# Moving the first half of one projection ahead of the last modulation chunks in a two-block transformer kernel

## The reference, cut to what matters

```python
mod = jax.nn.silu(c) @ w_mod[l] + b_mod[l]                     # (1, 6 * 1024)
sh_m, sc_m, gt_m, sh_f, sc_f, gt_f = [m[:, None, :] for m in jnp.split(mod, N_MOD, axis=-1)]

h = rms_norm(x, g_mix_norm[l]) * (1.0 + sc_m) + sh_m
proj = h @ w_in[l]
(q_a, k_a, v_a, q_i, k_i, w_i, q_b, k_b, v_b, gate_a, gate_b) = jnp.split(proj, split_at, axis=-1)
...
q_i = apply_rope(q_i.reshape(B, S, IDX_HEADS, IDX_DIM), cos_i, sin_i)
k_i = apply_rope(k_i[:, :, None, :], cos_i, sin_i)[:, :, 0, :]
w_i = w_i * idx_w_scale
...
q_b = apply_rope(rms_norm(q_b.reshape(B, S, MOBA_HEADS, HEAD_DIM), g_q_moba[l]), cos_h, sin_h)
k_b = apply_rope(rms_norm(k_b.reshape(B, S, MOBA_HEADS, HEAD_DIM), g_k_moba[l]), cos_h, sin_h)
```

## Time and profile before

| | |
|---|---|
| median of 3 runs | 1490.16 us (1490.03 to 1490.28) |
| profiled execution, its own time | 1494.77 us |
| its span | 1492.7 us |
| TensorE busy | 1450.2 us, 97% of the span |
| VectorE, ScalarE busy | 849.1 us, 689.3 us |
| mean granted TensorE clock | 0.99 |
| read from HBM | 269.19 MB |

### The profile page before, as it was taken

One profiled execution on the slowest core, in us unless ns is written; L12 is line 12 of the kernel. 1 busy time (PEld: TensorE's weight loads), 2 busy tenths in 40 slices (PEclk: granted clock), 3 DMA queues, 4 the chain that ended last, 5 costly groups with the idle time before them and its releaser, 6 DMA issues.

```text
span 1492.7 us, 17981 instructions
## 1 busy us (share of the span) xinstructions
PE 1450.2 (97%) x6910; PEld 1161.4 (78%) x6910; DVE 849.1 (57%) x1033; ACT 689.3 (46%) x880; POOL 36.1 (2%) x53
## 2 busy tenths in 40 slices
PE   6999999999999999999999999999999998999998
PEld 3757777788888888888888888788888865788887
DVE  2687766554556545466755455565445658655444
ACT  2454454444344444454454444754444667554442
POOL 0010100000000000000000000200000020000000
PEclk9999999999999999999999999999999989999999
DMA  9763767455564655546555655555555510455551
GB/s 343 272 224 113 244 222 264 133 196 187 179 196 156 211 179 187 194 157 200 182 177 189 188 179 196 148 191 178 195 184 183 191 41 29 141 178 189 190 190 70
DMA packets 188163, 271.13 MB, mean 182 GB/s; under 512 B 8380, under 2 KB 134148, under 8 KB 188100
## 3 DMA queue, kind: packets, MB, share of 16 engines
q1 hardware_dynamic: 186448, 267.01, 54.3%
q10 hardware_dynamic: 1492, 2.98, 0.7%
q0 software_dynamic: 160, 0.26, 0.2%
HBM read 269.19 MB, written 1.05 MB: 181 GB/s over the span
## 4 chain that ended last, share of the span: by engine, by line
PE 84%; DVE 6%; ACT 3%; DMA 3%; issue 2%; SPq 1%; POOL 0%; ACTq 0%; DVEq 0%
PE bank L1821 25%; PE bank L1823 25%; PE bank L1822 25%; DVE w_lo_ring L1327 2%; PE bank L1851 2%; DMA raw_ring<-in_w_mod_dram 1%; ACT w_hi_ring L982 1%; PE bank L1991 1%; DMA raw_ring<-in_w_in_dram 1%; PE bank L2123 1%; PE bank L2045 1%; PE bank L2144 1%; SPq L885 1%; PE bank L1879 0%; PE bank L1959 0%
## 5 line engine op out<-in xcount | busy, mean ns | idle before, releaser
L1327 DVE TENSOR_TENSOR w_lo_ring<-raw_ring,w_hi_ring 128x2048 fp32r<-128x2048 f32 (+1 forms) x226 | 513.8, 2277 | 401.6 <-ACT w_hi_ring L1270 329.8
L1821 PE MATMUL bank<-w_hi_ring,h_hi 128*128 128x512 f32 x1360 | 543.5, 400 | 2.2 <-DVE h_lo L1475 1.0
L1823 PE MATMUL bank<-w_hi_ring,h_lo 128*128 128x512 f32 x1360 | 531.8, 391 | 0.0
L1822 PE MATMUL bank<-w_lo_ring,h_hi 128*128 128x512 f32 x1360 | 530.9, 390 | 0.0
L1270 ACT ACTIVATE w_hi_ring<-raw_ring 128x2048 fp32r<-128x2048 f32 x158 | 302.8, 1917 | 295.8 <-PE bank L1823 292.5
L1821 PEld LDWEIGHTS bank<-w_hi_ring,h_hi 128*128 128x128 f32 x1360 | 256.2, 188 | 66.5 <-issue 15.6
L1823 PEld LDWEIGHTS bank<-w_hi_ring,h_lo 128*128 128x128 f32 x1360 | 255.8, 188 | 54.9
L1822 PEld LDWEIGHTS bank<-w_lo_ring,h_hi 128*128 128x128 f32 x1360 | 256.4, 189 | 49.4
L1821 PE MATMUL bank<-w_hi_ring,f_hi 128*128 128x512 f32 (+1 forms) x456 | 177.1, 388 | 0.0
L1823 PE MATMUL bank<-w_hi_ring,f_lo 128*128 128x512 f32 (+1 forms) x456 | 176.0, 386 | 0.0
L1822 PE MATMUL bank<-w_lo_ring,f_hi 128*128 128x512 f32 (+1 forms) x456 | 175.7, 385 | 0.0
(11 more groups left out here) (259 smaller groups left out, 873.1 us busy)
## 6 DMA issues: line engine op xcount, KB each, us to landing
raw_ring<-in_ffn_w_gate_up_dram SPq DMA_DIRECT2D x176, 512.0 KB
raw_ring<-in_ffn_w_down_dram SPq DMA_DIRECT2D x44, 1024.0 KB
raw_ring<-in_w_in_dram SPq DMA_DIRECT2D x22, 1024.0 KB
raw_ring<-in_w_gate_up_dram SPq DMA_DIRECT2D x44, 512.0 KB
arena<-in_w_mod_dram SPq DMA_DIRECT2D x18, 1024.0 KB, 7.1
raw_ring<-in_w_down_dram SPq DMA_DIRECT2D x11, 1024.0 KB
raw_ring<-in_conv_w_in_dram SPq DMA_DIRECT2D x16, 512.0 KB
raw_ring<-in_w_mod_dram SPq DMA_DIRECT2D x6, 1024.0 KB
```

The source lines that it names most:

```text
L1327: dve.tensor_tensor(w_lo[:, u % RING, 0:words], raw[:, r % RING, 0:words], w_hi[:, u % RING, 0:words].bitcast(F32), ALU.subtract).then_inc ...
L1821: pe.matmul(dst, hi, whi, start=start, stop=False)
L1822: pe.matmul(dst, hi, wlo, start=False, stop=False)
L1823: return pe.matmul(dst, lo, whi, start=False, stop=stop)
```

## The change

The first half of `qb` moves ahead. `qi`'s first half is cut in four pieces of one k-tile, with chunk 3's two products behind the third and fourth; then come four pieces of `qb`'s first half, with the products of chunk 1 behind the first, and the sums of chunks 3 and 1 behind the second. `xh` groups 2 and 3 follow. `warm` is gone. `qb` takes pair 1 for itself, `ki` the third pair, and `kb`, `vb` and the gates each change to the other pair; the extra count ahead of `bb`'s second chunk, which kept the pairs of the later stages, is dropped. The split of `qi`'s second half stands between chunk 1's products and the sums, on ScalarE and VectorE. Behind `qi`, the modulation items of chunks 5 and 6 come about one unit of weights later than before. The gains are issued after `xh` group 3, and the tables move from ScalarE's queue to SyncE's, behind the load of `qi`'s second half.

```diff
-THIRD = {("bb", 1): -1, ("qg", 1): -2}
+THIRD = {("ki", 0): -3, ("bb", 1): -1, ("qg", 1): -2}
...
-    plan.extend(xh[:2] + mod_load(3) + mod_load(1) + mod_rows(3))
-    part("qi", 0, 0, 2, [mod_sum(1), [dict(kind="warm", times=10)], mod_a[1:], [dict(kind="then split", unit=1 - RING)], xh[2:]],
-         [mod_sum(3) + mod_row(1, 0), mod_row(1, 1)])
+    plan.extend(xh[:2])
+    add("then split", unit=1 - RING)
+    plan.extend(mod_load(3) + mod_load(1))
+    part("qi", 0, 0, 2, [], [[], [], mod_row(3, 0), mod_row(3, 1)], held=True)
+    second = [dict(kind="then split", unit=2 - RING)]
+    part("qb", 0, 0, 2, [], [mod_rows(1) + second, mod_sum(3) + mod_sum(1) + mod_a[1:], xh[2:], []], held=True)
+    add("then split", unit=3 - RING)
     part("qi", 0, 1, 2, [evac("qi"), mod(4, 0)])
     part("ki", 0, 0, 1, [mod_row(4, 0), evac("ki"), mod(4, 1)])
-    part("qb", 0, 0, 2, [mod_row(4, 1), [dict(kind="kir")], mod(5, 0)], [[dict(kind="tp", stage="kiu", g=0)], []])
-    part("qb", 0, 1, 2, [mod_sum(4), tgroup("qi", 2), tgroup("ki", 1), mod_row(5, 0), evac("qb"), mod(5, 1)])
-    part("kb", 0, 0, 2, [mod_row(5, 1), mod(6, 0)])
-    part("kb", 0, 1, 2, [mod_sum(5), tgroup("qb", 2), mod_row(6, 0), evac("kb"), mod(6, 1)], [index[0], [], index[1], index[2]])
+    part("qb", 0, 1, 2, [mod_row(4, 1), mod(5, 0), [dict(kind="kir")], mod_sum(4), tgroup("qi", 2), evac("qb")],
+         [[], [dict(kind="tp", stage="kiu", g=0)]])
+    part("kb", 0, 0, 2, [tgroup("ki", 1), mod_row(5, 0), mod(5, 1)])
+    part("kb", 0, 1, 2, [mod_row(5, 1), mod(6, 0), mod_sum(5), tgroup("qb", 2), evac("kb")], [index[0], [], index[1], index[2]])
...
-    part("vb", 0, 0, 2, [mod_row(6, 1)], [[], index[3], index[4], index[5] + rot[0]])
-    part("vb", 0, 1, 2, [mod_sum(6), evac("vb")], [rot[1], index[6], index[7], rot[2]])
+    part("vb", 0, 0, 2, [mod_row(6, 0), mod(6, 1)], [[], index[3], index[4], index[5] + rot[0]])
+    part("vb", 0, 1, 2, [mod_row(6, 1), mod_sum(6), evac("vb")], [rot[1], index[6], index[7], rot[2]])
...
-            if item["stage"] == "bb" and item["chunk"]:
-                number("pi")
...
+                if raws[r] == ("unit", find["unit", "qi", 0]):
+                    sp.dma_start(const[:, C_COSH:], A["const"][:, C_COSH:]).then_inc(sem("tables_full"), 16)
...
-                if k == "xh" and g == 1:
+                if k == "xh" and g == 3:
                     for i, g in enumerate(("g_q_dsa", "g_k_dsa", "g_q_moba", "g_k_moba")):
                         act.dma_start(gains[:, i, :], A[g].to_broadcast([P, HD])).then_inc(sem("gains_full"), 16)
-                    act.dma_start(const[:, C_COSH:], A["const"][:, C_COSH:]).then_inc(sem("tables_full"), 16)
...
-                if k == "warm":
-                    pe.wait_ge(sem("xh_done"), 2)
-                    for _ in range(item["times"]):
-                        pe.matmul(bank[2][:, 0:256], ident, const[:, 0:256], start=True, stop=True)
```

## The result

The changed kernel took 1497.51 us (median of 5 runs, 1495.57 to 1499.99); the kernel before, beside it, 1490.16. The ratio is 1.005 (95% interval 1.0038 to 1.0063): slower by some 7.3 us, above the predicted range.

The account below looks back on a forecast made before the run. TensorE, busy 1450.2 of 1492.7 us, gains only where it waits, repeats itself or runs slow. 7.2 - 3.9 - 2.1 - 1.1 + 0.5 - 1.2 = -0.6: 1490.8 us, no measurable change; range 1486.8 to 1494.0.

Parts of the forecast that it names:

- Steps 1 to 4: Up to `kb`'s first product: `qi`'s second half at 44.6, `qb`'s at 58.0, `kb` at 71.3; lead left 0.1 us.
- step 3: Clock after the wait before `qb`'s second half: slow stretch covers 4.2 us of products, -2.1 us.
- step 5: From `kb` to `vb`: ScalarE and VectorE start on `kb` 1.6 us earlier, of which TensorE gains +0.5 us.
- Step 6: Behind `vb`: chunk 6's row copy follows the index-score scaling, then sum, `ga` products and transposes in line: -1.2 us.
- step 1: First product to `qi`'s second half: starts at 44.6 not 46.3, `qb` products worth 5.5 done, TensorE ahead 7.2 us.
- The carrying over: Difference at the first product behind the `kb` transposes, 0.6 us slower, carried unchanged to the kernel's end.
- A: Rival, faster: TensorE's own work bounds, waits give way; first product behind `kb` transposes before 109.7; 1486.4 us, chance 0.18.
- C: Rival, slower: chunk 1's transfer stays the bound, `qi`'s second half at about 48; 1494.2 us, chance 0.08.
- B: Rival, slower: clock stays slow in `qi`'s first half (1.7) and longer before `qb`'s second half (1.3); 1493.8 us, chance 0.16.
- step 2: Before `qb`'s second half: TensorE waits for VectorE's low split behind `qi`'s rotation, 54.1 to 58.0, -3.9 us.

Follow-up runs that it names:

- the second profile: Kernel before, unchanged, profiled once more: 1490.24 us (1 run), first product behind the `kb` transposes at 109.89 us.
- a wait filled alone: The change with five unused products ahead of chunk 6's sum only: 1497.12 us, again 1495.71; with seven before `qb`'s second half only: 1496.17.

## Why the prediction was wrong

- **Steps 1 to 4, against the profile they were read from**, came out: 44.88 for 44.6, 58.22 for 58.0, 71.01 for 71.3. The slow stretch of step 3 cost 1.7 us: `qb`'s second half took 7.2 us (58.22 until `kiu` at 65.43) for 24 products of 0.23, against 2.1 predicted. The 0.5 that step 5 added is not there: at `vb`'s end TensorE was 0.2 us ahead (107.78 against 107.98), predicted 0.6.
- **Step 6 failed: it put the slow clock behind its wait at nothing.** It had the row copy behind the scaling and the sum behind the copy, and placed that sum at 110.2 (110.50). Then it went on with 0.95, 1.4 and 0.8 at full clock. Measured are 1.6, 2.7 and 1.56 from start to start: 5.84 instead of 3.15, and 0.5 more until the clock is back at 117.4. Step 3 had charged a slow clock for a gap of 3.9 us; the gap of 2.71 here got none. From 0.2 us ahead TensorE fell 4.2 behind: the step is -4.4, not -1.2. That this order, wait and slow clock together, costs the time is shown by the two pairs of kernels that differ in the place of that row alone.
- **The lead of step 1 was read from one execution, and was too large for others.** 2.8 of its 7.2 us are the later start of `qi`'s second half behind a slow `warm` (46.28 against 43.52), which the second profile doesn't have; against that one the lead is 4.4. The prediction saw that its profiled execution was 4.6 us above the median, carried the difference over all the same, and so counted an excess as a gain: it lay in the very stretch that the change removes. A gain there could not also be subtracted from the median.
- Put together: -0.6 predicted, -0.4 up to `vb`, -3.2 in step 6 are the -4.2 that the first profile shows behind 118 us; -2.8 for `warm` makes -7.0, which the second profile shows there (6.45 at the first product, and the 0.5), and the times differ by 7.3.
- **The carrying over held.** From 118 us to the slow stretch at 236 to 248, the starts of the same VectorE instructions keep their distance to either profile of before within 0.4 us; against the first, which has that stretch slow as the change has, they keep it until 1160 us. The condition that the prediction named for its being wrong there (all steps as written, and yet over 3 us) was not the one that came true.
- **Rivals.** A fell (the first product was to start before 109.7). C fell: chunk 1's products, both halves, ran without a wait from 36.30 on, and the transfers moved 410 GB/s from 25.0 to 28.0 us, where they had 257 before. B named the clock, but at other places: it was 0.95 in the first half of `qi` from 28.4 to 31.8 in the changed kernel's profile, and the slow stretch behind the wait of step 2 was shorter, not longer, than assumed. That the clock could fall behind `vb` stood in no rival.

The Trainium skill, "TensorE: Matmul & The Clock Gate", section "HAM oscillation — how this bites in real kernels", says that products which wait in every round for their operand, some 3 to 5 us in its example, start each round slow. No run here has such rounds; the single waits of that length agree in part: behind 3.81 us at 58 five products still ran at the full clock and then the slow ones came, and behind 4.63 in the kernel with `qb`'s split earlier the sum was slow at once. The wait of 2.71 at 110 is shorter than the page's, and the clock fell there too, so here the measurement goes beyond the page.

The prediction weighed the slow clock at one of its two waits only.

What stays open: why a wait filled alone gains 2.85 us in the trace and nothing that shows in the time, why the earlier row gains 8.7 us of the time and 5.3 of the span, and which executions get a slow stretch at 236 to 248 and beyond 1200 us. No run here tells what decides it.

## What to carry to other kernels

A small copy that TensorE waits for belongs ahead of the long item in VectorE's queue, not behind it; when an item is moved, look at what will then stand before each copy on the engine that makes it. Price a wait of TensorE as the wait and the slow products that may follow it, and ask for these at every wait and not only at the longest: here they followed 2.71 us as well as 3.81 and 4.63, and not 1.42. And if the profiled execution is longer than the median, find where its excess lies before an edit there is given credit for it.

## What was not expected of the hardware

The wait of 2.71 us ahead of the sum of chunk 6 was followed by a clock of 0.54 over 7.4 us, while 1.42 at the same place before left it at 1.00 (the stretch from 110 in the first profile), and 2.73 in the kernel with `qb`'s split earlier gave 0.77. `warm`, which was to keep the clock up, ran mostly at the slow clock in one execution (7.1 us until the next product) and at the full one in another (4.2) of the same kernel. And one unchanged order of work can lose about 1.7 us at 236 to 248: of the two profiles of the kernel before one did and one didn't.
